# Dilated-attention layer: turning the q and k tiles of two dilations by DMA transposes instead of on TensorE

## What is computed

```python
for gi, (window, dil) in enumerate(((128, 1), (512, 4), (2048, 16))):
    q = partial_rope(proj[:, :, gi, 0], cos, sin)
    k = partial_rope(proj[:, :, gi, 1], cos, sin)
    v = proj[:, :, gi, 2]
    o, lse = banded_attention(to_residue(q, dil), to_residue(k, dil), to_residue(v, dil), window // dil)
# the three outputs are mixed by softmax over their lse, then multiplied by w_o
```

## Time and profile before

| | |
|---|---|
| median of 3 runs | 810.12 us (810.08 to 810.49) |
| the profiled execution, its own time | 810.76 us |
| its span, first to last instruction | 809.0 us |
| PE busy | 798.6 us (99%) |
| DVE busy | 528.5 us (65%) |
| ACT busy | 457.5 us (57%) |
| POOL busy | 102.2 us (13%) |
| mean granted TensorE clock | 0.997 |

### The profile page before, as it was taken

The page is one execution under the profiler, slowest core; times in us unless marked ns, Lnnn a source line. Parts: engine busy times, 40 slices in busy tenths (PEclk is TensorE's granted clock), DMA queues, the critical chain, the costliest instruction groups (busy, mean ns, idle before and its releaser), DMA issues.

```text
span 809.0 us, 11869 instructions
## 1 busy us (share of the span) xinstructions
PE 798.6 (99%) x4401; PEld 643.8 (80%) x4401; DVE 528.5 (65%) x1121; ACT 457.5 (57%) x879; POOL 102.2 (13%) x167
## 2 busy tenths in 40 slices
PE   9999999999999999999999999999999999999996
PEld 7877675788888888788888888888877888888885
DVE  6966969796565556697566665766668775655644
ACT  7836877765444444575555566555658554444431
POOL 1000005812212221000000000000000112222210
PEclk9999999999999999999999999999999999999998
DMA  9955211168886687658544535363424688678811
GB/s 318 351 184 200 86 54 53 59 189 241 242 212 191 191 238 216 188 198 269 157 157 153 160 121 192 105 208 105 157 88 172 191 248 224 173 197 236 236 21 52
DMA packets 128490, 142.24 MB, mean 176 GB/s; under 512 B 25856, under 2 KB 111920, under 8 KB 128304
## 3 DMA queue, kind: packets, MB, share of 16 engines
q1 hardware_dynamic: 107760, 132.53, 52.6%
q10 hardware_dynamic: 19680, 4.75, 3.6%
q0 software_dynamic: 992, 4.19, 1.4%
HBM read 134.64 MB, written 2.10 MB: 169 GB/s over the span
## 4 chain that ended last, share of the span: by engine, by line
PE 96%; DVE 2%; ACT 1%; issue 0%; POOL 0%; ACTq 0%; POOLq 0%
PE ps L1830 86%; PE ps L1839 6%; PE ps L2107 2%; PE ps L2080 2%; PE ps L2118 1%; PE ps L1892 1%; ACT junk L756 0%; DVE w_lo L1256 0%; ACT xd_hi L744 0%; ACT w_hi L735 0%; ACT probs_b L907 0%; DVE h L1580 0%; DVE h L1586 0%; DVE tmp L1584 0%; ACT p_t L922 0%
## 5 line engine op out<-in xcount | busy, mean ns | idle before, releaser
L1256 DVE TENSOR_TENSOR w_lo<-w_raw,w_hi 128x1024 fp32r<-128x1024 f32 x240 | 295.5, 1259 | 64.8 <-ACT w_hi L735 62.5
L735 ACT ACTIVATE w_hi<-w_raw 128x1024 fp32r<-128x1024 f32 x240 | 245.5, 1060 | 3.0 <-DMA w_raw<-in_ffn_w_gu 2.9
L1830 PE MATMUL ps<-w_hi,xt_hi 128*128 128x512 f32 x472 | 188.5, 401 | 0.3 <-ACT w_hi L735 0.3
L1830 PE MATMUL ps<-w_hi,xt_lo 128*128 128x512 f32 x472 | 183.5, 390 | 0.0
L1830 PE MATMUL ps<-w_lo,xt_hi 128*128 128x512 f32 x472 | 183.0, 390 | 0.0
L1830 PE MATMUL ps<-w_hi,xd_hi 128*128 128x512 f32 x288 | 117.4, 408 | 0.2 <-DVE w_lo L1256 0.2
L1830 PE MATMUL ps<-w_hi,xd_lo 128*128 128x512 f32 x288 | 113.2, 393 | 0.0
L1830 PE MATMUL ps<-w_lo,xd_hi 128*128 128x512 f32 x288 | 112.8, 392 | 0.0
L1830 PEld LDWEIGHTS ps<-w_hi,xt_hi 128*128 128x128 f32 x472 | 88.5, 188 | 25.0 <-issue 8.6
L1830 PEld LDWEIGHTS ps<-w_hi,xt_lo 128*128 128x128 f32 x472 | 88.6, 188 | 18.9
L1830 PEld LDWEIGHTS ps<-w_lo,xt_hi 128*128 128x128 f32 x472 | 88.7, 188 | 16.7 <-DVE w_lo L1256 0.3
(11 more groups left out here) (271 smaller groups left out, 984.9 us busy)
## 6 DMA issues: line engine op xcount, KB each, us to landing
w_raw<-in_ffn_w_gu SPq DMA_DIRECT2D x88, 512.0 KB, 5.6
w_raw<-in_dil_w_in SPq DMA_DIRECT2D x72, 512.0 KB, 4.6
w_raw<-in_ffn_w_down SPq DMA_DIRECT2D x44, 512.0 KB, 5.4
w_raw<-in_nsa_w_in SPq DMA_DIRECT2D x20, 512.0 KB, 7.3
w_raw<-in_nsa_w_o SPq DMA_DIRECT2D x8, 512.0 KB, 4.8
w_raw<-in_dil_w_o SPq DMA_DIRECT2D x8, 512.0 KB, 4.5
w_k<-in_nsa_cmp_wk SPq DMA_DIRECT2D x2, 1024.0 KB, 9.0
w_raw<-in_nsa_cmp_wv SPq DMA_DIRECT2D x2, 1024.0 KB, 11.5
```

The costliest lines, as they stand in the source:

```text
L735: act.activation(w_hi[:, n.slot, c:c + 1024], w_raw[:, n.slot, c:c + 1024], ACT.Copy)\
L1256: dve.tensor_tensor(w_lo[:, n.slot, c:c + 1024], w_raw[:, n.slot, c:c + 1024], w_hi[:, n.slot, c:c + 1024].bitcast(F32), ALU.subtract)\
L1830: ins = pe.matmul(o, s, m, start=start, stop=stop, **kw)
```

## The change

It takes the QK tiles of patterns 0 and 1 (16 of 24) off PE's transposes. `split_qk` on POOL copies a roped tile into two 16-bit planes (128 x 1024 halves, twice the size of the feed-forward's), `dil_planes` on ACT issues one DMA transpose for them, `merge_qk` on POOL puts the halves together into `qk_t`, in token order. The planes lie in `h`, which is in DRAM at that time; so `h` is saved in two halves and loaded back only after the last merge. Since tokens stay in order, the scores read q and k of pattern 1 with a stride of four numbers, and k of pattern 0 with a stride of two. High and low parts of pattern 0 are made once per group by four steps between ACT and DVE (`first_q_hi`, `first_lo_out`, `first_k_hi`, `first_lo_out`). The factor -SCALE moves into the mask operation.

```diff
+            def split_qk(x):
+                pool.wait_ge(roped[1], x.qk_no + 1)
+                pool.tensor_copy(view(planes_q, BARS.index(x) % 2 * 1024, [[512, 2], [1, 512]]),
+                                 halves_of(stage_dil[:, x.qk_no % 2, :])).then_inc(planes_ready, 1)
+            def merge_qk(x):
+                i, pos = BARS.index(x), qk_order(x.g).index(x.pat)
+                pool.wait_ge(planes_turned[i % 2], 16 * (xbar_of(0, FJ - 2, i % 2) + i // 2 + 1))
+                if x.g - (pos == 0) > 0:
+                    pool.wait_ge(scores[1], 8 * (x.g - (pos == 0)))
+                to = qk_t[:, qk_slot(x.g, x.pat), :, x.m * P:(x.m + 1) * P].bitcast(U16)
+                pool.tensor_copy(to.rearrange("p b (i k) -> p k b i", k=2),
+                                 view(planes_qt, i % 2 * 1024, [[512, 2], [P, 4], [1, P]])).then_inc(ht_merged, 1)
...
+                    save_h(0)
                     pool.wait_ge(h_saved, 16)
+                    save_h(1)
...
+                    for g in range(DIL_G):
+                        first, second, third, fourth = [x for x in BARS if x.g == g]
+                        split_qk(first)
+                        split_qk(second)
+                        merge_qk(first)
+                        split_qk(third)
+                        merge_qk(second)
+                        split_qk(fourth)
+                        merge_qk(third)
+                        merge_qk(fourth)
+                    pool.wait_ge(ht_merged, len(XBAR) + DIL_BARS)
                     pool.dma_start(h[:, :, :], h_rows.rearrange("(p m) c -> p m c", m=MT)).then_inc(h_permuted, 16)
...
+            def dil_planes(x):
...
+                act.wait_ge(planes_ready, bar_at(x) + 1)
+                act.dma_start_transpose(planes_qt[:, i % 2, :, :], planes_q[:, i % 2, :])\
+                   .then_inc(planes_turned[i % 2], 16)
             def dil_turn_out(x):
-                if x.kind != QK:
+                if x not in PE_TURNS:
                     return
...
+            def first_q_hi(g):
+                act.wait_ge(ht_merged, len(XBAR) + 4 * (g + 1))
+                for hp in range(2):
+                    ins = act.activation(first_q_part(q_hi, hp), first_q_whole(g, hp), ACT.Copy)
+                ins.then_inc(qk_hi_ready, 1)
+            def first_k_hi(g):
+                act.wait_ge(qk_lo_ready, 2 * g + 1)
+                at = qk_slot(g, 0)
+                act.activation(k_parts[:, at, 0, :, :], qk_t[:, at, 2:4, :], ACT.Copy).then_inc(qk_hi_ready, 1)
...
                 dil_evac(TILES[e - 1])
                 split(n + k, (0,))
+                if TILES[e].g > TILES[e - 1].g:
+                    first_q_hi(TILES[e - 1].g)
                 dil_attend(2 * e)
                 dil_odd_out(2 * e + 1)
...
+                if TILES[e].g > TILES[e - 1].g:
+                    first_k_hi(TILES[e - 1].g)
+                dil_planes(TILES[e - 1])
                 dil_turn_out(TILES[e - 1])
...
+            def first_lo_out(g):
+                dve.wait_ge(qk_hi_ready, 2 * g + 1)
                 for hp in range(2):
+                    ins = dve.tensor_tensor(first_q_part(q_lo, hp), first_q_whole(g, hp),
+                                            first_q_part(q_hi, hp).bitcast(F32), ALU.subtract)
                 ins.then_inc(qk_lo_ready, 1)
+                at = qk_slot(g, 0)
+                dve.wait_ge(qk_hi_ready, 2 * g + 2)
+                dve.tensor_tensor(k_parts[:, at, 1, :, :], qk_t[:, at, 2:4, :], k_parts[:, at, 0, :, :].bitcast(F32),
+                                  ALU.subtract).then_inc(qk_lo_ready, 1)
...
             def dil_turn(x):
-                if x.kind != QK:
+                if x not in PE_TURNS:
                     return
...
             def dil_scores(g, t):
...
                 if t == 0:
-                    pe.wait_ge(qk_lo_ready, 2 * (g + 1))
+                    pe.wait_ge(ht_merged, len(XBAR) + 4 * (g + 1))
+                    pe.wait_ge(turn_out[1], 2 * (g + 1))
...
-                                     head(g, pat, 0, j, m * P + 64 * cls, 64), head(g, pat, 1, j, m * P + c, 64, 2),
-                               True, True)
+                               class_q(g, pat, j, m, cls), class_k(g, pat, j, m, c), True, True)
+                if t == 0:
+                    pe.wait_ge(qk_lo_ready, 2 * (g + 1))
```

More of the change, by code:

```diff
@@ L119, with bar_at @@
 XBAR = [(1, 0), (1, 1)] + [(j, m) for j in range(2, FJ - 1) for m in range(MT)]
+DIL_BARS = 2 * MT * DIL_G
 def xbar_no(layer, j, m):
-    return len(XBAR) * layer + XBAR.index((j, m))
+    return (len(XBAR) + DIL_BARS) * layer + XBAR.index((j, m))
 def xbar_of(layer, j, m):
     tiles = [x for x in XBAR if x[1] == m]
-    return len(tiles) * layer + tiles.index((j, m)) + 1
+    return (len(tiles) + DIL_BARS // 2) * layer + tiles.index((j, m)) + 1
 TILES = dil_tiles()
 LAST_E = len(TILES)
-N_TURNS = sum(x.kind == QK for x in TILES)
-def firsts_until(qk_no):
-    return sum(x.kind == QK and x.pat == 0 and x.qk_no <= qk_no for x in TILES)
+BARS = [x for x in TILES if x.kind == QK and x.pat < 2]
+PE_TURNS = [x for x in TILES if x.kind == QK and x.pat == 2]
+def bar_at(x):
+    return len(XBAR) + BARS.index(x)
 def pair_start(g, t):
@@ L299, in build @@
         p_t2 = sb("p_t2", [P, 2, 512], at=at_s + 4096)
-        qk_lo = [sb(f"qk_lo{i}", [P, S], F32R, at=at) for i, at in
-                 enumerate((at_gp + 3072, at_s + 9216, at_tmp + 3072, at_tmp + 7168))]
+        q_hi, q_lo = ([sb(f"q_{k}{hp}", [P, S], F32R, at=at) for hp, at in enumerate(homes)] for k, homes in
+                      (("hi", (at_gp + 3072, at_s + 9216)), ("lo", (at_tmp + 3072, at_tmp + 7168))))
         mask_nsa = sb("mask_nsa", [P, 2 * P], BF16, at=at_s + 9216)
@@ L661, in _ @@
                 p2 = mask_dil[rows, 0, 257 - cls:DIL_N:2]
-                link(pool.affine_select(out=p1, in_=p1, compare_op=ALU.is_ge, fill=-NEG,
+                link(pool.affine_select(out=p1, in_=p1, compare_op=ALU.is_ge, fill=NEG / SCALE,
                                         base=0, pattern=[[-1, 64]], channel_multiplier=1))
-                link(pool.memset(p2, -NEG))
+                link(pool.memset(p2, NEG / SCALE))
                 for d in range(0, 64, 4):
@@ L699, in turn_hidden, with save_h @@
                     merge_hidden(layer, j, m)
+            def split_qk(x):
[10 more added lines that the diff above has]
+                                 view(planes_qt, i % 2 * 1024, [[512, 2], [P, 4], [1, P]])).then_inc(ht_merged, 1)
+            def save_h(m):
+                for half in range(2):
+                    pool.wait_ge(h_ready[2][half], m + 1)
+                pool.dma_start(h_rows[m * P:(m + 1) * P, :], h[:, m, :]).then_inc(h_saved, 16)
             for b in range(1, 4):
@@ L1201, in _ @@
             split(n + 3, (0,))
+            first_q_hi(DIL_G - 1)
+            first_k_hi(DIL_G - 1)
             dil_turn_out(TILES[-1])
@@ L1447, in cmp_probs, with mask_part @@
                    .then_inc(pc_ready, 1)
-            def mask_part(dst, w, c, n, mask, least):
-                return dve.tensor_tensor_reduce(out=dst, in0=bank(score_bank(w), c, n), in1=mask, scale=1.0,
+            def mask_part(dst, w, c, n, mask, least, scale=1.0):
+                return dve.tensor_tensor_reduce(out=dst, in0=bank(score_bank(w), c, n), in1=mask, scale=scale,
                                                 scalar=INF, op0=ALU.add, op1=ALU.min, accum_out=least)
```

115 lines of the change are left out of this document (57 added, 58 removed).

## The result

The changed kernel takes 815.43 us (median of 4 executions, 814.03 to 816.04); the kernel before took 810.31 us beside it (4 executions). The ratio is 1.0059, with a 95% interval of 1.0042 to 1.0077: slower, by 5.1 us in the medians. The profiled execution took 814.03 us over a span of 812.3 us, at a mean granted TensorE clock of 0.999.

A forecast was written before the change was run, and what follows sets the result against it. PE was taken to bound the kernel, busy for 96% of the span; -6.4 for removed turns, +6.7 for four waits and +0.6 at the end made +0.9 us, so 811.0 us, with eight in ten from 805.0 to 816.0.

The forecast's parts named there:

- the forecast's own case: Whole kernel: PE waits at four places, 1.3 to 2.2 us each, giving 809.4 to 813.0 us; chance 0.42.
- the prediction's own signs: Signs of being wrong: PE's waits stand elsewhere, a score block grows from 0.94 us, or POOL is late with a merge.
- Removed turns, -6.4: On PE: sixteen turns of q/k tiles removed at 0.40 us each, 6.4 us less (5.6 to 7.2).
- The 0.35 us for a turn beside probabilities: On PE: four transposes cost 0.35 us where probabilities are turned just ahead, against 0.45 us elsewhere.
- Strided reads, 0: PE's score matmuls: 16-byte steps in pattern 1 and 8-byte steps in pattern 0's k cost nothing.
- bounds that summed to 8.3: Half-rate reads in PE's sixteen score blocks: 3.2 us for pattern 1 plus 5.1 us for pattern 0's fp32r reads.
- the rival with a chance of 0.14: Strided reads slow PE's score matmuls: 3.2 or 8.3 us on top of the forecast, 814.2 to 819.3 us; chance 0.14.
- Four waits, +6.7: PE waits 1.68 us for ACT's copy of probabilities, late behind plane copy and issue, at four places: 6.7 us.
- Issue, 1.95 us: On ACT: a DMA transpose issue for 1024 columns grows with size to 1.95 us; ends 1.21 and 2.41.
- Landing, 7 to 8 us: DMA transposes of twice the size land some 7 to 8 us after issue; below 9.9 us this costs nothing.
- ACT becoming the bound: Rival, steps 13 to 16 and 31 to 34: ACT bounds or DMAs land late; +7.0, 817.1 us; chance 0.14.
- The end, +0.6: After the last tile: PE waits 0.6 us ahead of group 3's scores for the ACT and DVE chain of parts.

The follow-up runs named there:

- run 8: Changed kernel with POOL's merge writing sorted columns, normalization ahead of the rope, and ACT's last turn-out ahead of the k part; 804.32 us, ratio 0.9918 to the kernel before.
- Run 12: Changed kernel with ACT's last turn-out ahead of the k part, plus pattern 1's q in unit and k in 8-byte steps (wrong columns); 811.48 us.
- run 2: Changed kernel with pattern 0's k read in unit steps (keys in another order than the mask's); 809.57 us, ratio 0.9986 to the kernel before.
- run 4: Changed kernel with DVE normalizing the even unit ahead of the rope instead of behind it; 812.68 us, ratio 1.0025 to the kernel before.
- run 1: The changed kernel measured again without edit; 814.58 us against 810.64 for the kernel before, ratio 1.0051.
- run 5: Changed kernel with only pattern 1's stationary q read in unit steps (wrong tokens), k still at 16 bytes; 814.68 us, ratio 1.0044 to the kernel before.
- runs 5 and 6: Run 5, and the changed kernel with only pattern 1's moving k narrowed from 16- to 8-byte steps (wrong tokens); the latter 815.77 us, ratio 1.0051.
- runs 1 to 4: Run 1, run 2, run 4, and the changed kernel with pattern 1's q and k both in unit steps (wrong columns); the last 812.07 us, ratio 1.0017.

## Why the prediction was wrong by 4 us and where it was right

The forecast was 811.0 us; 815.4 came, outside the forecast's own case (809.4 to 813.0), inside the wide range (805.0 to 816.0), on the side that had the largest chance. That it lies in the range is partly luck: the mechanism was another. By the prediction's own signs, a score block that grows and waits that stand elsewhere, it was wrong.

- **Removed turns, -6.4.** Right, and 0.6 us too small. By run 8 the change without its three side effects stands at 804.32 - 810.86 = -6.5 us, with 0.5 us of wait still in it: 7.0 us, inside the 5.6 to 7.2. The 0.35 us for a turn beside probabilities was a misreading of the earlier trace rows; it was 0.45 there too.
- **Strided reads, 0.** This is the step that failed: "I take nothing, as the nearest row runs at full speed". It was +7.7, of bounds that summed to 8.3. For fp32r the upper bound was exact: 0.32 us a block, half rate. For pattern 1 the block grew by 0.16 where the bound was 0.20. The nearest row was a plain fp32 matmul with 64 moving columns. Run 12 shows that its 8-byte step is indeed free there (0.39 us); the fp32r matmul of 256 columns has no such slack (run 2). The two differ in type, length and tile shape at once; which of these decides was not tested. A row that differed in all three was taken as the nearest, and "8 bytes are free" was held against the rival with a chance of 0.14 that came true (815.4 lies in its 814.2 to 819.3, though without most of the waits that it stood on). The rule of the Trainium skill that was weighed there (SBUF — State Buffer, "Door 1: The DMA port swizzle", lines of 16 bytes) pointed the right way for pattern 1, 3.2 us against 2.5 measured; by it pattern 0's step of 8 bytes, two numbers in a line, would have been free, and the trace has 5.0 us there. The measurement decides.
- **Four waits, +6.7.** Right in number and pairs, wrong in cause and place and mis-sized: 2.0 by the trace, 1.9 by run 4. ACT's copy of probabilities was not late, since plane copy and issue took 1.04 + 1.25 us, below the 2.6 at which the prediction itself let the wait vanish; in tile 13 that copy ended at 426.74, and PE turned the odd unit at 427.38. In its place PE's turn of the even unit, half a tile earlier, came late, because DVE's normalization stood behind POOL's plane copy. The prediction had looked at that contention only for what it does to POOL's copy, not for what it does to DVE. The normalization stands between the two rows, just where a copy that starts at 424.30 would meet it:

```profile
424.54 0.42 DVE L1484 TENSOR_SCALAR probs_dil<-probs_dil,rl 128x384 f32<-128x384 f32 x1
```

- **Issue, 1.95 us.** It took 1.25 for twice the columns, against 1.21: size hardly counts. The growth with size that was inferred from the Trainium skill (DMA: Bandwidth & Descriptors, "Why a DMA increments its semaphore by 16 and not by 1") is 0.04 us here.
- **Landing, 7 to 8 us.** It took 4.4 in the median, 9.3 at most, below the 9.9 of room. The value was too high, but what it was to decide is right: PE waited for no merge. ACT becoming the bound did not come either.
- **The end, +0.6.** 1.3 us. The chain was the right one, but I gave strided copies their unstrided durations: ACT's two q copies took 1.22 us instead of 0.66, DVE's two 1.13 instead of 0.76.
- **Moved load and save of `h`, mask.** Nothing, as said.

So the size came as near as it did by errors of opposite sign, and that is luck: 7.7 us left out and 0.7 us too little at the end on one side, 4.7 us of waits too much and 0.6 us of turns too little on the other. They sum to +3.1, from the +0.9 forecast to about the +3.95 us of the traces, which run 1 repeats in its medians (3.94). The first measurement's 5.1 us hold besides two executions of four at a mean clock of 0.996, 815.95 and 816.04, beside 814.03 at 0.999; neither has a trace, so that the dip of run 5 is behind them is likely but not shown.

## What to carry to other kernels

When a change turns a layout step into a strided read, price the read at half rate until a row with the same type, operand and shape shows otherwise (here half rate was exact for one pattern and the upper bound for the other), and look whether an engine with time to spare can write in the sorted order instead: here POOL did it for 4.4 us of its own time and gave PE 7.7 back. When work is given to an idle POOL, look which DVE instruction starts just behind it, and who waits for that one; the cure may be to swap two lines of DVE's list. When two variants are to be told apart by half a microsecond, read the block that was changed in the trace, since the clock can move the total by more.

## What the hardware showed that I had not expected

- A step of 8 bytes in the moving operand of a 256-column fp32r matmul took the last pair from 0.21 to 0.34 us and the six from 0.54 to 0.86; the same step in a 64-column plain fp32 matmul cost nothing (0.39 us for sixteen records).
- A step of 16 bytes costs on either side of the 64-column plain fp32 matmul, and the sides do not add: 0.39 us with neither, 0.49 (moving k), 0.52 (stationary q), 0.55 (both). q's step shows in the weight load, 133 to 172 ns in the mean of both patterns, 177 with k's.
- ACT and DVE feel 16-byte steps of their SBUF reads too: a copy or subtraction of 128 x 256 took 664 and 606 ns with 16 bytes, 430 and 420 with 8.
- A DMA transpose of 128 x 1024 halves holds ACT's queue for 1.25 us, one of 128 x 512 for 1.21.
- A DVE instruction that started 0.17 us behind a POOL copy ended 0.21 us after it, 1.08 us for 0.42; weight splits that overlapped a POOL merge by 0.78 and 1.28 us both ended 1.02 us after it.
- After PE had stood for 1.25 us, TensorE's clock was at 1.2 GHz from about 2 us later on for some 3 us in the profiles of runs 5 and 6, and stayed at 2.4 GHz in those of runs 1 to 4.
